# Attention outputs of a head pair formed together from kept turned probabilities, with the top-k rounds placed elsewhere

## What is computed

```python
for l in range(DEPTH):                       # DEPTH = 2, x: 512 x 1024
    proj = rms_norm(x, norm1[l]) @ w_in[l]
    # four groups of 4 heads: A (latent), B (window of 128), C (top-k keys), D (forget gates)
    o_a = causal_block_attention(q_a, k_a, v_a, 96 ** -0.5)
    o_b = sliding_window_attention(q_b, k_b, v_b, swa_sinks[l], 64 ** -0.5)
    o_c = dsa_attention(q_c, k_c, v_c, qi, ki, c_w, 128, 64 ** -0.5)
    o_d = causal_block_attention(q_d, k_d, v_d, 64 ** -0.5, log_f_cum=cum)
    x = x + concatenate([o_a, o_b, o_c, o_d]) @ w_out[l]
    h2 = rms_norm(x, norm2[l])
    x = x + square(relu(h2 @ w_up[l])) @ w_down[l]
```

## Time and profile before

| | us |
|---|---|
| median of 3 runs | 1915.2 |
| lowest, highest | 1913.44, 1916.31 |
| the profiled execution | 1912.91 |
| its span, first to last instruction | 1911.1 |

### The profile page before, as it was taken

One profiled execution on the slowest core, in us unless ns is written; L12 is line 12 of the kernel. 1 busy time (PEld: TensorE's weight loads), 2 busy tenths in 40 slices (PEclk: granted clock), 3 DMA queues, 4 the chain that ended last, 5 costly groups with the idle time before them and its releaser, 6 DMA issues.

```text
span 1911.1 us, 22949 instructions
## 1 busy us (share of the span) xinstructions
PE 1844.5 (97%) x9010; PEld 1470.6 (77%) x9010; DVE 907.8 (48%) x1555; ACT 651.2 (34%) x1174; POOL 740.1 (39%) x330
## 2 busy tenths in 40 slices
PE   7999889999999999998999999999899999999997
PEld 6678557888888886776577888888788988888786
DVE  3667871414141426688724543526512124339374
ACT  4533452312121245443523121212434443442212
POOL 5232342444344443332524445445333333234342
PEclk9999899999999999998999999999999999999999
DMA  7224002222322233120014334242332223222221
GB/s 223 67 67 165 2 23 66 89 88 88 107 91 88 72 93 109 45 86 3 23 63 162 120 142 154 89 174 88 94 121 88 66 67 110 91 67 89 88 66 44
DMA packets 104441, 170.89 MB, mean 89 GB/s; under 512 B 21615, under 2 KB 39431, under 8 KB 103208
## 3 DMA queue, kind: packets, MB, share of 16 engines
q1 hardware_dynamic: 103320, 169.79, 27.2%
q10 hardware_dynamic: 1040, 0.00, 0.0%
HBM read 166.56 MB, written 7.93 MB: 91 GB/s over the span
## 4 chain that ended last, share of the span: by engine, by line
PE 88%; DVE 7%; ACT 2%; issue 2%; DMA 0%; POOL 0%; SPq 0%; DVEq 0%; ACTq 0%
PE G L2033 26%; PE G L2035 25%; PE G L2034 25%; PE S L2295 2%; DVE neg_max L1905 1%; PE S L1059 1%; DVE select L1869 1%; ACT prob L1512 1%; PE S L2078 1%; PE S L1033 1%; PE G L2331 1%; DVE work L1705 1%; PE S L1044 1%; PE G L2312 1%; DVE top L1704 1%
## 5 line engine op out<-in xcount | busy, mean ns | idle before, releaser
L1289 POOL TENSOR_TENSOR w_lo<-raw,w_hi 128x1024 fp32r<-128x1024 f32 x268 | 668.0, 2513 | 1011.6 <-ACT w_hi L1335 690.2
L1335 ACT ACTIVATE w_hi<-raw 128x2048 fp32r<-128x2048 f32 x94 | 180.0, 1915 | 542.2 <-PE G L2035 542.2
L2033 PE MATMUL G<-h_hi,w_hi 128*128 128x512 f32 x896 | 359.8, 402 | 2.7 <-DVE h_lo L816 2.7
L2035 PE MATMUL G<-h_hi,w_lo 128*128 128x512 f32 x896 | 354.6, 396 | 0.0
L2034 PE MATMUL G<-h_lo,w_hi 128*128 128x512 f32 x896 | 354.5, 396 | 0.0
L2033 PE MATMUL G<-w_hi,h_hi 128*128 128x512 f32 (+2 forms) x704 | 280.5, 398 | 3.7 <-issue 2.0
L2035 PE MATMUL G<-w_hi,h_lo 128*128 128x512 f32 (+2 forms) x704 | 271.3, 385 | 0.0
L2034 PE MATMUL G<-w_lo,h_hi 128*128 128x512 f32 (+2 forms) x704 | 271.3, 385 | 0.0
L2035 PE MATMUL G<-w_hi,u_lo 128*128 128x512 f32 x512 | 204.4, 399 | 0.0
L2033 PEld LDWEIGHTS G<-h_hi,w_hi 128*128 128x128 f32 x896 | 168.5, 188 | 45.4 <-DVE h_lo L816 3.5
L2034 PE MATMUL G<-w_lo,u_hi 128*128 128x512 f32 x512 | 201.9, 394 | 0.0
(11 more groups left out here) (316 smaller groups left out, 2213.2 us busy)
## 6 DMA issues: line engine op xcount, KB each, us to landing
raw<-in_w_in_dram SPq DMA_DIRECT2D x40, 1024.0 KB, 5.4
raw<-in_w_up_dram SPq DMA_DIRECT2D x32, 1024.0 KB, 5.2
raw<-in_w_down_dram SPq DMA_DIRECT2D x32, 1024.0 KB, 5.0
raw<-in_w_out_dram SPq DMA_DIRECT2D x12, 1024.0 KB, 5.0
w_ada<-in_w_ada_dram SPq DMA_DIRECT2D x4, 3072.0 KB, 11.9
skew_scratch<-line_scratch SPq DMA_DIRECT2D x1, 4608.0 KB
raw<-in_w_in_dram SPq DMA_DIRECT2D x8, 512.0 KB, 4.5
raw<-in_w_in_dram SPq DMA_DIRECT2D x4, 832.0 KB, 6.7
```

The source lines that it names most:

```text
L1289: ins = pool.tensor_tensor(w_lo[:, c % SPLIT_SLOTS, part], raw[:, c % RAW_SLOTS, part], w_hi[:, c % SPLIT_SLOTS, part].bitcast(F32), ALU.s ...
L1335: act.activation(w_hi[:, c % SPLIT_SLOTS], raw[:, c % RAW_SLOTS], ACT.Copy).then_inc(high_ready, 1)
L2033: pe.matmul(dst, a_hi, b_hi, start=first, stop=False)
L2035: return pe.matmul(dst, a_lo, b_hi, start=False, stop=last)
```

## The change

1. Outputs are formed for a whole pair at once, for the first five pairs: eight matmuls, key tile by key tile, of 512, 384, 256 and 128 columns (a key tile serves all query tiles from its own on), one of each for each head. The last pair keeps one output for each item. There are nine outputs in a layer in place of 24. `give_output` of a pair stands in TensorE's loop at the second item of the next pair, ahead of `give_probs(i - 1)`, where an item's output stood behind it.
2. Turned probabilities are kept for the pair: `probT` becomes two tiles, one for each head (`probT_83` and `probT_88` in the order below), of 2048 columns. Key tile k of query tile t lies at 384 k + 128 t, so that the copies (`turned_tiles`) write tiles 384 columns apart. The second tile lies where `rows_b` begins. The copies wait for the previous pair's output before they write.
3. The copies of the outputs out of PSUM go from VectorE (24 of 128 columns) to ScalarE (five of 512 and four of 128 columns), behind `take_probs`.
4. Rounds: `EARLY_ROUNDS` 36, `EARLY_STEPS` 21: the 22 calls beside the projections now do 1, 2, 2, 1, 2, 2, 2, 1, 2, 2, 1, 2, 2, 2, 1, 2, 2, 1, 2, 2, 2, 0 rounds (before 1, 1, 2, 1, 1, 2, 1, 2, 1, 1, 2, 1, 2, 1, 1, 2, 1, 2, 1, 1, 2, 1). The other 12 are at items 3, 7, 11 and 15 (two each) and 4, 8, 12 and 16 (one each).
5. `MIX_ORDER` puts the two D tiles ahead of the first C tile, and VectorE's splits at the end wait for the outputs.

```diff
-MIX_ORDER = (0, 1, 2, 3, 4, 6, 7, 5)
+MIX_ORDER = (0, 1, 2, 3, 6, 7, 4, 5)
...
-EARLY_ROUNDS = 2 * ROUNDS
-EARLY_STEPS = side_steps(1, NS + 1)
+LAST_PAIR = len(PAIRS) - 1
+OUTPUTS = [(p, None) for p in range(LAST_PAIR)] + [item for item in ITEMS if item[0] == LAST_PAIR]
+LAYER_OV = len(OUTPUTS)
+PT_STEP = (TT - 1) * P
+EARLY_ROUNDS = 9 * ROUNDS // 4
+EARLY_STEPS = side_steps(1, AT["M",]) - 1
+def late_rounds(i):
+    return {3: 2, 0: 1 if i else 0}.get(i % TT, 0)
...
+        def output_of(i):
+            p = ITEMS[i][0]
+            if p == LAST_PAIR:
+                return LAST_PAIR + i % TT
+            return p if i % TT == TT - 1 else None
...
-        def output_bank(i):
-            return [G[HD * e:HD * e + HD, 2 + i % 2, 0:P] for e in range(2)]
+        def output_bank(o, first, end):
+            return [G[HD * e:HD * e + HD, 3 - o % 2, first:end] for e in range(2)]
+        def turned_tiles(i, e):
+            qt = ITEMS[i][1]
+            return probT[e][:, P * qt:P * qt + PT_STEP * (qt + 1)].rearrange("p (k n) -> p k n", n=PT_STEP)[:, :, 0:P]
...
                 def take_probs(i):
                     act.wait_ge(turn_filled, turns + (PT_NO[i, 1] + 1))
-                    if i >= 2:
-                        act.wait_ge(o_filled, item0 + (i - 1))
-                    act.activation(probT[:, i % 2, 1, 0:width], G[:, 1, 0:width], ACT.Copy).then_inc(odd_drained, 1)
+                    if ITEMS[i][0]:
+                        act.wait_ge(o_filled, out0 + ITEMS[i][0])
+                    act.activation(turned_tiles(i, 1), fresh_tiles(i, 1), ACT.Copy).then_inc(odd_drained, 1)
+                def take_output(o):
+                    p, qt = OUTPUTS[o]
+                    first, end = (0, SEQ) if qt is None else (P * qt, P * qt + P)
+                    act.wait_ge(o_filled, out0 + (o + 1))
+                    act.activation(mixed(*PAIRS[p])[:, first:end], G[:, 3 - o % 2, first:end], ACT.Copy
+                                   ).then_inc(o_drained, 1)
...
                         take_probs(i - 1)
+                    if i > 1 and output_of(i - 2) is not None:
+                        take_output(output_of(i - 2))
...
-                    if i > 1:
-                        take_output(i - 2)
-                    top_rounds(2 if i < 4 else 1)
+                    top_rounds(late_rounds(i))
...
                 def give_output(i):
-                    for b, kb in enumerate(tiles):
-                        for e, dst in enumerate(output_bank(i)):
-                            ins = pe.matmul(dst, values(p, e, kb), probT[:, i % 2, e, P * b:P * b + P],
+                    tiles = range(TT) if qt is None else key_tiles(i)
+                    for kb in tiles:
+                        first, end = (P * kb, SEQ) if qt is None else (P * qt, P * qt + P)
+                        for e, dst in enumerate(output_bank(o, first, end)):
+                            ins = pe.matmul(dst, values(p, e, kb), probT[e][:, PT_STEP * kb + first:PT_STEP * kb + end],
...
                         give_scores(i + 1)
+                    pair_done = i > 1 and i - 2 < LAST_PAIR * TT and output_of(i - 2) is not None
+                    if pair_done:
+                        give_output(i - 2)
                     if 0 < i <= NI:
                         give_probs(i - 1)
-                    if i > 1:
+                    if i - 2 >= LAST_PAIR * TT:
                         give_output(i - 2)
```

More of the change, by code:

```diff
@@ L180 @@
 LAYER_SC = NB + NI
-LAYER_OV = NI
-EARLY_ROUNDS = 2 * ROUNDS
-EARLY_STEPS = side_steps(1, NS + 1)
+LAST_PAIR = len(PAIRS) - 1
[6 more added lines that the diff above has]
+    return {3: 2, 0: 1 if i else 0}.get(i % TT, 0)
+assert EARLY_ROUNDS + sum(late_rounds(i) for i in range(4 * TT + 2)) >= 3 * ROUNDS
 assert LAYER_TURNS % 2 == 0
@@ L408, in build @@
         prob = room.place("prob", [P, 2, 2, SEQ])
-        probT = room.place("probT", [P, 2, 2, SEQ])
+        probT = [room.place("probT0", [P, TT * SEQ])]
         assert room.at <= free_at
@@ L417, in build @@
         rows_b, rows_c = room.place("rows_b", [P, TT, 512]), room.place("rows_c", [P, TT, 512])
+        probT.append(Room(nc, xn_at).place("probT1", [P, TT * SEQ]))
         early = Room(nc, room.at)
@@ L1554, in _ @@
                         if k == 0:
-                            act.wait_ge(o_drained, item0 + (4 * TT + PAIR_CREDIT))
+                            act.wait_ge(o_drained, out0 + (4 + PAIR_CREDIT))
                             act.wait_ge(even_taken, evens + EVENS)
                         high_mix(k)
-                act.wait_ge(o_drained, item0 + (5 * TT + PAIR_CREDIT))
+                act.wait_ge(o_drained, out0 + (5 + PAIR_CREDIT))
                 for k in MIX_ORDER[HALF_K:KT - 1]:
                     high_mix(k)
-                act.wait_ge(o_drained, item0 + (NI + PAIR_CREDIT))
+                take_output(LAYER_OV - 1)
+                act.wait_ge(o_drained, out0 + (LAYER_OV + PAIR_CREDIT))
                 high_mix(MIX_ORDER[KT - 1])
@@ L1678, in _ @@
             for l in range(DEPTH):
-                unit, tr, item0, score0 = l * LAYER_UNITS, l * LAYER_TR, l * NI, l * LAYER_SC + NB
+                unit, tr, out0, score0 = l * LAYER_UNITS, l * LAYER_TR, l * LAYER_OV, l * LAYER_SC + NB
                 turns, evens = l * LAYER_TURNS, l * EVENS
@@ L1709, in mark @@
                     step.done(dve.tensor_scalar(chosen(qt), left, TAKEN * 0.9, NEG, ALU.is_gt, ALU.mult))
-                rounds = iter(range(EARLY_ROUNDS + ROUNDS))
+                rounds = iter(range(3 * ROUNDS))
                 round_steps = itertools.count()
@@ L1717, in top_rounds @@
                         k = next(round_steps)
+                        if k >= EARLY_STEPS:
+                            return
                         count = (k + 1) * EARLY_ROUNDS // EARLY_STEPS - k * EARLY_ROUNDS // EARLY_STEPS
-                        if k == EARLY_STEPS - 1:
-                            return
                     for r in itertools.islice(rounds, count):
@@ L1952, in _ @@
                     if i == NI - 1:
+                        dve.wait_ge(turn_filled, turns + (PT_NO[NI - 2, 1] + 1))
                         split_mix(0, 2)
@@ L1956, in _ @@
                         split_mix(2, HALF_K)
-                split_mix(HALF_K, KT)
+                dve.wait_ge(o_filled, out0 + LAYER_OV - 2)
+                split_mix(HALF_K, HALF_K + 2)
+                dve.wait_ge(o_filled, out0 + LAYER_OV)
+                split_mix(HALF_K + 2, KT)
                 def add_to_x(first_unit, col, scale=None, tiles=range(TT)):
@@ L2322, in give_output @@
                 def give_output(i):
-                    p = ITEMS[i][0]
-                    tiles = key_tiles(i)
+                    o = output_of(i)
+                    p, qt = OUTPUTS[o]
                     turns_taken(PT_NO[i, 1])
-                    pe.wait_ge(o_drained, item0 + (i + 1))
-                    for b, kb in enumerate(tiles):
-                        for e, dst in enumerate(output_bank(i)):
-                            ins = pe.matmul(dst, values(p, e, kb), probT[:, i % 2, e, P * b:P * b + P],
-                                            start=b == 0, stop=b == len(tiles) - 1)
+                    pe.wait_ge(o_drained, out0 + (o + 1))
+                    tiles = range(TT) if qt is None else key_tiles(i)
[3 more added lines that the diff above has]
+                            ins = pe.matmul(dst, values(p, e, kb), probT[e][:, PT_STEP * kb + first:PT_STEP * kb + end],
+                                            start=kb == 0, stop=kb == tiles[-1])
                     ins.then_inc(o_filled, 1)
```

23 lines of the change are left out of this document (9 added, 14 removed).

## The result

| | us |
|---|---|
| kernel before, median of 4 runs (lowest, highest) | 1915.3 (1913.4, 1916.3) |
| changed kernel, median of 4 runs (lowest, highest) | 1936.2 (1931.4, 1938.5) |
| ratio | 1.0107, 95% interval 1.0092 to 1.0121 |
| profiled execution of the changed kernel, its span | 1934.15, 1932.4 |

The account below looks back on a forecast made before the run. TensorE, busy 97% of the span, bounds the kernel, with hand-overs setting the attention stage's end. Terms -4.3 - 0.6 + 2.4 + 2.05 + 2.4 + 1.3 + 1.3 = +4.55 us a layer, +9.1 on 1915.2: 1924 us, range 1909 to 1938.

Parts of the forecast that it names:

- the sum: Attention stage and projections: gains and losses add to +4.55 us a layer, +9.1 for two layers; forecast 1924 us, chance 0.50.
- head: Start of the attention stage: without early rounds TensorE's 2.21 us wait goes and two scores run at full clock, -4.3 us.
- pairs: Attention stage, first four pairs: 17.7, 17.7, 15.7 and 15.1 us; changes -0.6, +2.4, +2.05 and +2.4 us.
- tail: End of the attention stage: fifth pair's outputs wait for a ScalarE copy and hold back the next ones; +1.3 us a layer.
- the wait: First unit of a pair: TensorE waits 2.2 us for VectorE's turned copy behind two rounds, where it waited next to nothing.
- The start of the unit: TensorE's first unit of a pair starts 8.2 us after the fourth item's 512-wide scores end, before 7.54.
- the outputs: A pair's outputs on TensorE take 2.35 us together, 0.25 us less work, but stand where nothing else is waited for.
- the projections: Ahead of attention: more early rounds make VectorE's copy late for TensorE's window output, a stall of +1.3 us a layer.
- the first pair: First pair of the attention stage: 18.26 us with the low clock becomes 17.7 at the full one, -0.6 us.
- The clock: Rival, chance 0.16: TensorE's clock falls in the head as before, +6.7 us a layer, 1937.7 us.
- Faster: Rival, chance 0.16: VectorE's two rounds end before TensorE asks, unit starts at 7.5 us or sooner; -6.5 a layer, 1902 us.
- Nothing to measure: Rival, chance 0.18: late items find inputs ready, so losses are half, 4.1 for 8.15 us a layer; 1915 to 1917 us.

Follow-up runs that it names:

- filled versions: Changed kernel with fourteen products, or eight transposes, added on TensorE ahead of the first unit of the third to fifth pair: 1924.8 and 1926.9 us.
- singles: Kernel before with only its rounds spread: 33 beside the projections, one at each of items 1 to 15, outputs as before: 1904.0 us, ratio 0.9937.
- behind_singles: Changed kernel with 33 rounds beside the projections, one at each of items 1 to 15, and pair outputs behind the turned probabilities: 1914.6 us.
- pairs_singles: Changed kernel with 33 rounds beside the projections and one at each of items 1 to 15, pair outputs still ahead of the turned probabilities: 1918.1 us.

## Why the prediction was half right

**At the full clock the sum held.** The lengths that it gives (head 11.8, pairs 17.7, 17.7, 15.7 and 15.1, tail 18.9) can be read where no fall adds to them, in the changed kernel and its filled versions: 11.95, 17.76, 17.76, 15.59, 15.22 and 19.13. Two of these (the first and third pair of layer 0, at 206 and 243) hold a fall that costs nothing: it lies ahead of the wait for VectorE, which shrinks from 2.0 to 0.94 and 0.98 us. Of these, only the falls behind a wait cost time. The start of the unit (8.24 for 8.2), the wait (2.0 for 2.2), the outputs (2.30 for 2.35) and the projections (1.4 and 0.9 for 1.3) are as the steps put them. Two of the lengths are luck in part: the fourth pair's 15.1 had no steps behind it, and the tail's 1.3 was picked from 0 to 2.4 without a row. The projections' stall is where I had it, for VectorE's copy of `prob_b`:

```profile
846.97 0.66 PE L2254 MATMUL S<-rows_b,prob_b 128*128 128x64 f32 x4 [0.86 <-DVE prob_b L1872]
```

**The step that failed is the clock.** I booked a gain from it in both layers. In the head it was 2.2 us ("saves 0.35 more at the next units if the clock holds, and 1.8 on the two scores"), and in the first pair it was 2.9, the difference of 18.26 to the 15.33 us that such a pair takes at the full clock in `singles`. These 10.2 us were taken as saved, and nothing was put against them in the later pairs. In the changed kernel layer 0's head did hold; layer 1's, behind the same three short waits (0.43, 0.56 and 0.60 us), fell at 881.8 and stayed down for 20.5 us, and five falls stood behind the new waits. By the lengths above, half clock cost the stages 14.4 us in the changed kernel (4.6 and 9.8). In the kernel before it cost 13.2: 5.1 in each layer, and 1.6 and 1.4 us for the falls at 256.8 and 284.2. So the clock made 1.2 us of loss where I had 10.2 of gain. These 11.4 us are nearly the whole of the 12.2 between my sum (9.1) and the difference of the spans (21.3); the rest is in the tails, the fourth pair and the head.

**The rival.** "The clock", with 0.16 and 1937.7 us, has the cause, and the time came out within 1.5 us of it; that nearness is luck. Its 1937.7 stood for falls in the heads of both layers and none in the later pairs. What happened is a fall in one head (5.4 us with the first pair) and five behind the new waits (9.0 us). My reason against it was the 1.78 us between transposes at 697.23, with the clock at 1.00. That row is one case of one kind; 874.36, which I had as well, was the nearer one: the same engine pair, the same stage, the same length, and a fall right behind it in both layers. Nor was the row at 697.23 harmless: the same wait (1.77 or 1.78 us), between the same transposes, stands in all 14 profiled executions, and in four of them a fall begins 0.8 to 1.8 us after it. In `behind_singles` it looks so (the second fence is a stretch, columns as in the earlier trace rows, with the clock at 0.50):

```profile
695.07 3.02 PE L2107 MATMUL S<-masks,X 128*128 128x128 f32 x16 [1.78 <-DVE h_lo L1696]
```

```profile
697.00:699.00 2.00, 2.00 (x11) 2.00 (x10) 2.00 (x4) 1.58 (x4) 1.27 (x1) 0.50 0.00 0
```

So one execution without a fall could not say that such a wait is safe. In the stages of all profiled executions here TensorE waits 1.5 us or more 24 times (1.58 to 2.21), and 22 of these waits have a fall behind them (it begins from 0.3 us before the end of the wait to 2.3 us after it). I had put the row that suited the sum above the row of the place. Ranges and chances that treat the clock as one of four cases were too mild: the forecast's own new waits had the length that brings it about.

**The other rivals.** "Faster" was decided where I put it: the unit started at 8.24 and not at 7.5. "Nothing to measure" assumed that late items find their inputs ready and lose half as much; at the full clock no pair shows it.

**The outputs.** I had their mechanism (they filled waits before, and now stand where nothing waits), but as a part of one sum with the rounds. By the medians the runs give it a size of its own, 11 to 14 us with single rounds and 17 with the old ones, more than the 10 of the rounds alone.

## What to carry to other kernels

Work that is spread in small pieces between waits is worth more than the same work in one piece, even when the one piece has fewer instructions: before you gather it, list the waits that it fills. Spread background work on an engine that another one waits for: one round at each step cost less than a microsecond a layer here (the fourth pair, 13.56 us for 12.71), where two in a row at four places of a layer cost 10 us in all. And price a new wait of TensorE by what stands behind it at half clock too: take the nearest wait of the same length in the same stage, not one that was harmless elsewhere in a single execution.

## What the runs showed of the hardware

- A wait of TensorE of 1.6 to 2.2 us in the attention stage was followed by a fall of the clock to 1.2 GHz in 22 of 24 cases. In the later pairs of the changed kernel such a fall lasted 3.4 us and cost 1.2 to 1.6 us beside the wait (once 6.9 us and 3.0). In the head, where more short waits follow, it lasted 17.1 or 23.9 us. What sets the other two cases apart, or the ten of 14 executions in which the wait of 1.78 us between the transposes of the input had no fall behind it, no run here shows.
- Falls came behind short waits too: in the head behind three of 0.4 to 0.6 us (6.8 to 20.5 us long), in the later pairs behind two of 0.7 and 0.8 us, and in other pairs and executions the same waits had none. Where a fall lay ahead of a wait for another engine, it took up the wait and cost nothing.
- Runs of one kernel differ by the clock. The ten runs of `pairs_singles` go from 1911.35 us at a mean clock of 0.993 to 1923.14 at 0.983.
- Transposes kept the clock up as products did: eight (0.87 us) in a wait of 2 us were enough in four of four cases, with 1.14 us of it left empty.
- Outputs of 512 columns for two heads of 64 rows each stream together as those of 128 columns did (1.02 us for eight): 2.30 us for 2560 columns in all (920.10 to 922.40), where two 512-wide scores take 1.7 us for 1024.
- A copy of turned probabilities into tiles 384 columns apart took the same 0.68 us for 512 columns as the one into adjacent tiles.
